# In the head, GpSimd takes the low part of the first half of each weight piece

## The reference, cut to what matters

```python
mod = silu(c) @ mod_w + mod_b                 # shift, scale and gate, 2048 each
h = rms_norm(x, gain) * (1 + scale) + shift
u, v = split(gelu(h @ w_in), 2)               # w_in: 2048 x 8192
v = rms_norm(v, v_gain)                       # then mixed over tokens by w_s, masked to be causal
```

## Time and profile before

| | us |
|---|---|
| median of 3 runs | 2571.34 (2571.24 to 2572.14) |
| the profiled execution, its own time | 2566.57 |
| its span, first to last instruction | 2564.8 |
| TensorE (PE) busy | 2492.9, 97% |
| VectorE (DVE) busy | 2131.3, 83% |
| ScalarE (ACT) busy | 1241.6, 48% |
| GpSimd (POOL) busy | 339.2, 13% |

### The profile page before, as it was taken

The page is one execution under the profiler, slowest core; times in us unless marked ns, Lnnn a source line. Parts: engine busy times, 40 slices in busy tenths (PEclk is TensorE's granted clock), DMA queues, the critical chain, the costliest instruction groups (busy, mean ns, idle before and its releaser), DMA issues.

```text
span 2564.8 us, 38496 instructions
## 1 busy us (share of the span) xinstructions
PE 2492.9 (97%) x14006; PEld 2151.4 (84%) x14006; DVE 2131.3 (83%) x2587; ACT 1241.6 (48%) x1644; POOL 339.2 (13%) x190
## 2 busy tenths in 40 slices
PE   6999999998999999999999999899999999999999
PEld 4877888887888888888887888688788888888887
DVE  7899898999999889988998788679999756765666
ACT  3437343544554355534544344573555445543553
POOL 0000110231120011101130000363122001200110
PEclk8999999999999999999999999999999999999999
DMA  9999688886878877787777879208677655555554
GB/s 369 364 359 345 252 338 328 321 325 257 310 283 305 331 293 290 290 339 291 274 268 279 313 277 351 99 18 327 239 287 292 223 189 190 187 189 188 181 180 148
DMA packets 94023, 685.49 MB, mean 267 GB/s; under 512 B 10433, under 2 KB 10433, under 8 KB 11201
## 3 DMA queue, kind: packets, MB, share of 16 engines
q1 hardware_dynamic: 93170, 677.08, 70.4%
q10 hardware_dynamic: 720, 6.57, 0.6%
HBM read 681.51 MB, written 2.10 MB: 267 GB/s over the span
## 4 chain that ended last, share of the span: by engine, by line
PE 75%; DVE 8%; DMA 3%; issue 2%; ACT 2%; POOL 1%; DVEq 0%; SPq 0%; ACTq 0%
PE banks L1504 48%; PE banks L1508 24%; DMA raw<-in_stream 3%; DVE w_lo L1109 2%; POOL attn_area L700 1%; DVE raw L1125 1%; ACT w_hi L935 1%; DVE scratch L865 1%; DVE attn_area L663 0%; PE banks L1492 0%; DVE x_res L1227 0%; PE banks L796 0%; DVE temp L1251 0%; DVE zpad L1246 0%; PE banks L1523 0%
## 5 line engine op out<-in xcount | busy, mean ns | idle before, releaser
L935 ACT ACTIVATE w_hi<-raw 128x1024 fp32r<-128x1024 f32 x833 | 866.9, 1056 | 990.8 <-PE banks L1508 569.3
L1109 DVE TENSOR_TENSOR w_lo<-raw,w_hi 128x1024 fp32r<-128x1024 f32 x833 | 1079.7, 1318 | 315.8 <-ACT w_hi L935 313.1
L1504 PE MATMUL banks<-h_op,w_hi 128*128 128x512 f32 x3808 | 1197.1, 396 | 5.7 <-DVE w_lo L1109 5.0
L1508 PEld LDWEIGHTS banks<-h_op,w_lo 128*128 128x128 f32 x3808 | 715.4, 188 | 169.1
L1508 PE MATMUL banks<-h_op,w_lo 128*128 128x256 f32 x3808 | 748.2, 278 | 0.0
L1504 PE MATMUL banks<-act_op,w_hi 128*128 128x512 f32 x2176 | 683.9, 396 | 0.8 <-DVE act_op L1269 0.5
L1504 PEld LDWEIGHTS banks<-h_op,w_hi 128*128 128x128 f32 x3808 | 579.7, 189 | 7.4 <-issue 4.6
L1125 DVE CUSTOM_DVE_ANT_0 raw<-raw,c_all 128x2048 f32<-128x2048 f32 x224 | 544.5, 2447 | 15.4 <-ACT c_all L909 9.6
L1508 PEld LDWEIGHTS banks<-act_op,w_lo 128*128 128x128 f32 x2176 | 408.8, 188 | 96.6
L1508 PE MATMUL banks<-act_op,w_lo 128*128 128x256 f32 x2176 | 427.5, 278 | 0.0
L1504 PEld LDWEIGHTS banks<-act_op,w_hi 128*128 128x128 f32 x2176 | 331.2, 189 | 1.7 <-DVE w_lo L1109 0.9
(11 more groups left out here) (159 smaller groups left out, 1312.3 us busy)
## 6 DMA issues: line engine op xcount, KB each, us to landing
raw<-in_stream SPq DMA_DIRECT2D x641, 1024.0 KB, 5.7
mix_area<-in_cmp_w ACTq DMA_DIRECT2D x2, 2048.0 KB, 11.7
x_res<-in_x SPq DMA_DIRECT2D x1, 2048.0 KB, 11.4
out_x<-x_res SPq DMA_DIRECT2D x4, 512.0 KB, 4.5
mix_area<-in_w_s ACTq DMA_DIRECT2D x1, 1024.0 KB, 10.2
mix_area<-in_b_s ACTq DMA_DIRECT2D x1, 1024.0 KB, 14.8
small<-in_small SPq DMA_DIRECT2D x1, 682.0 KB, 16.3
attn_area<-in_pos ACTq DMA_DIRECT2D x1, 273.0 KB, 5.3
```

The lines of the kernel that those rows point to most:

```text
L935: act.activation(w_hi[:, out, 0:n], raw[:, slot, half:half + n], ACT.Copy).then_inc(hi_ready, 1)
L1109: dve.tensor_tensor(w_lo[:, out, 0:n], raw[:, slot, half:half + n], w_hi[:, out, 0:n].bitcast(F32), ALU.subtract).then_inc(stream, 2 if ch ...
L1504: pe.matmul(banks[:, g + j, :], hi[:, k, P * j:P * (j + 1)], operand[:, kt, :], start=(kt == 0), stop=False, skip_group_check=True)
L1508: last = pe.matmul(banks[:, g + j, 0:T], lo[:, k, P * j:P * (j + 1)], operand[:, kt, 0:T], start=False, stop=(kt == last_kt), skip_group_c ...
```

## The change

In the head, `split_lo` on VectorE skips the first half of each weight piece (u even), and for the second half adds 2 to `stream`, so that a whole piece counts at once. GpSimd makes the low part of the first half, after `hi_ready`, and counts on a new semaphore `head_low`. TensorE waits for `head_low` ahead of a first half and for `stream` ahead of a second. The load of a piece waits for `stream` and, if the slot held a weight piece of the head, for `head_low` as well; for that the loads that follow pieces of the head are taken out of the loop and written out, with fixed addresses. The mask of `w_s` goes from ahead of GpSimd's steps to its first step of `sgu_u0`, behind the low parts.

```diff
@@ sync
+            head_pieces = BY_NAME["sgu_u0"][0].n["G"]
+            by_pool = [0] * head_pieces
+            for ch in BY_NAME["head"]:
+                for off, piece_kind in enumerate(ch.kinds_of):
+                    if piece_kind == "w":
+                        by_pool[ch.n["G"] + off] = 4 * ch.hs + ch.kinds_of[:off].count("w") + 1
             full = n_pieces // RAW_SLOTS
-            with sp.Fori(1, full) as i:
+            in_head = head_pieces // RAW_SLOTS + 1
+            for g in range(RAW_SLOTS, in_head * RAW_SLOTS):
+                sp.wait_ge(stream, 2 * (g - RAW_SLOTS + 1))
+                if by_pool[g - RAW_SLOTS]:
+                    sp.wait_ge(head_low, by_pool[g - RAW_SLOTS])
+                sp.dma_start(raw[:, g % RAW_SLOTS, :], io["stream"][g * P:(g + 1) * P, :]) \
+                    .then_inc(raw_loaded[g % RAW_SLOTS], 16)
+            with sp.Fori(in_head, full) as i:
@@ vector, split_lo
+                in_head = PHASE_OF[id(cur.first)] == "head"
+                if in_head and u % 2 == 0:
+                    return
...
-                                  ALU.subtract).then_inc(stream, 2 if chunk.kind == "gate" else 1)
+                                  ALU.subtract).then_inc(stream, 2 if in_head or chunk.kind == "gate" else 1)
@@ gpsimd
-            pool.wait_ge(mix_loaded, 32)
-            pool.affine_select(out=w_sT, in_=w_sT, compare_op=ALU.is_ge, fill=0.0, base=0,
-                               pattern=[[0, SGU_G], [1, P]], channel_multiplier=-1).then_inc(masked, 1)
-
             def step(name, cur, prev, first):
+
+                if name == "head":
+                    for u in range(0, 8, 2):
+                        off = cur.first.piece_of[[i for i, t in enumerate(cur.first.tokens) if t == "s"][u]]
+                        slot, out = (cur.first.n["G"] + off) % RAW_SLOTS, (cur.first.n["S"] + u) % SPLIT_SLOTS
+                        pool.wait_ge(hi_ready, cur.first.n["S"] + u + 1)
+                        pool.tensor_tensor(w_lo[:, out, :], raw[:, slot, 0:SUB], w_hi[:, out, :].bitcast(F32),
+                                           ALU.subtract).then_inc(head_low, 1)
+                if name == "sgu_u0" and first:
+                    pool.wait_ge(mix_loaded, 32)
+                    pool.affine_select(out=w_sT, in_=w_sT, compare_op=ALU.is_ge, fill=0.0, base=0,
+                                       pattern=[[0, SGU_G], [1, P]], channel_multiplier=-1).then_inc(masked, 1)
@@ tensor
-                    pe.wait_ge(stream, cur.val(lambda c: 2 * (c.n["G"] + off) + u % 2 + 1))
+                    if name == "head" and u % 2 == 0:
+                        pe.wait_ge(head_low, 4 * cur.first.hs + u // 2 + 1)
+                    else:
+                        pe.wait_ge(stream, cur.val(lambda c: 2 * (c.n["G"] + off) + u % 2 + 1))
```

More of the change, by code:

```diff
@@ L353, in build @@
         hi_ready = sem("hi_ready")
+        head_low = sem("head_low")
         stream = sem("stream")
```

## The result

The changed kernel takes 2580.65 us (2579.34 to 2581.22) against 2571.33 us for the one before, a ratio of 1.0041 (95% interval 1.0029 to 1.0053): slower, by about 10 us. The ratios here are taken over all runs of both kernels, so they are not exactly the quotient of the two medians. Run again beside later kernels the ratio was 1.0053 (1.0040 to 1.0066). The profiled execution took 2579.65 us, its span is 2577.9, 13.1 more than before.

What follows compares the result with a forecast made beforehand. TensorE bounds the kernel, so only the head counts: 190.4 us shared path + 10 late pieces - 189.7 = +10.7, or 2577.3 profiled; 4.8 carried over to the median gives 2582 us. Own range 2572 to 2593; 8 in 10, 2572 to 2601.

Steps and rivals of the forecast that it cites:

- The price of the GpSimd operation: Head: each added GpSimd low part takes 2.21 us of a path shared with VectorE, against 1.14 replaced; full lock 2.41.
- The shared path: Head: low parts on both engines, modulation pieces and operand makings sum to 190.4 us in 189.7, additions covered; chance 0.64.
- The late pieces: Head: of 13.6 us VectorE waits for late weight pieces, three quarters, 10 us, stay; ends 0 and 14.
- the three makings: Head: three makings of the operand, each 8.67 us in place of 4.49 between modulation pieces, add 12.5 us.
- VectorE's standstill: Head sign: VectorE's low parts and modulation pieces stretched by some 2 us per pair, means above 1.3 and 2.3.
- relief: Rival, head: lock rarely bites, standstill under 1.14 us per operation; 11.5 us faster, 2560 us; chance 0.06.
- The replay: Head's first pairs stepped through: modulation piece ends at 46.0 (before 42.6), next half 47.1; slots return 1 to 3 us later.
- The loads' and TensorE's waits: Head: loads waiting for both engines add nothing; TensorE's later first half counts only at the start, 1.1 us inside the sum.
- The mask: Mask of w_s moved behind the head's low parts stops VectorE as long there: net zero, between -1.4 and +2 us.
- One to one: The head's lengthening or shortening shifts the long TensorE stretch from 270 to 2560 us as a whole; it absorbs nothing.
- the transfers: Rival, head: transfers set the pace at a 357 GB/s ceiling; 0 to +4 us, taken as 2573; chance 0.14.
- let in late: Rival, head: GpSimd operations wait for VectorE's and take 6.56 us each; +33 us, 2604; chance 0.16.

Runs made afterwards that it cites:

- the three later series: Follow-up experiments, each run against the kernel before on the same chip; that kernel measured 2566.43, 2566.34 and 2567.54 us.
- where it was isolated: Kernel before plus one GpSimd subtraction per head pair on unrelated data, result unused, only the mask waiting for it: 2613.94 us, ratio 1.0187.
- the two split kernels: Changed kernel with GpSimd low parts only in the 10 head pairs with additions (2563.78 us, 0.9993 to kernel before), or only in the 22 others (2578.11, 1.0050).
- the kernel that was only late: VectorE makes all low parts; TensorE and loads wait for a GpSimd memset after the first one: 2571.70 us, ratio 1.0018 to the kernel before.

## Why the prediction was right

The forecast was +10.7 us, 2582; the timed medians give +9.3, the profiled spans +13.1, and the medians beside the later kernels +13.9. So the loss is some 9 to 14 us, and direction and size were right. That 2582 and 2580.65 lie so near is in part luck: the forecast was carried over to a median of the kernel before, 2571.34, that stood 4 to 5 us above its medians in the three later series (2566.34 to 2567.54). By its steps:

- *The price of the GpSimd operation*, 2.21 us: 2.20 where it was isolated, not the whole 2.41.
- *The shared path*, 32 x 5.56 + 12.5 = 190.4 us: pairs in a row took 5.52 (41.52 to 47.04). With additions they took 5.55, 5.56 and 5.55:

```profile
222.48 2.28 DVE L1142 CUSTOM_DVE_ANT_0 raw<-raw,c_all 128x2048 f32<-128x2048 f32 x1
224.69 1.28 DVE L1165 TENSOR_TENSOR scratch<-banks,scratch 128x512 f32<-128x512 f32 x2
225.89 2.21 DVE L1126 TENSOR_TENSOR w_lo<-raw,w_hi 128x1024 fp32r<-128x1024 f32 x1
228.03 2.28 DVE L1142 CUSTOM_DVE_ANT_0 raw<-raw,c_all 128x2048 f32<-128x2048 f32 x1
...
233.59 2.28 DVE L1142 CUSTOM_DVE_ANT_0 raw<-raw,c_all 128x2048 f32<-128x2048 f32 x1
...
239.14 4.09 DVE L1142 CUSTOM_DVE_ANT_0 raw<-raw,c_all 128x2048 f32<-128x2048 f32 x1
```

  These pairs are no longer with an addition than without: GpSimd covers it, as assumed. It does not do so in all ten: laid over each other, the timelines leave 3.6 us of additions, of 12.8 in the head, beside which GpSimd does not work. The prediction put this at nothing. Here the pairs were 5.7 to 6.3 us before, so this end of the head lost nothing, which the two split kernels confirm.
- *The late pieces*, 10 us of 13.6. From GpSimd's first low part (38.16) to 241.35, where the last modulation piece would have ended without the mask behind it (239.14 + 2.21), it is 203.2 us. Less 32 x 5.55 and 12.7 for the three makings (9.78 each from modulation piece to modulation piece, 5.55 without), 12.9 stay. The same overlay of the timelines tells what they are: for 8.2 us, outside the makings, neither engine works; 3.6 are the uncovered additions; 1.1 is not accounted for. The longest such wait, 170.98 to 173.04, stands behind an uncovered addition, VectorE's lines first:

```profile
169.69 1.28 DVE L1165 TENSOR_TENSOR scratch<-banks,scratch 128x512 f32<-128x512 f32 x2
174.01 2.46 DVE L1126 TENSOR_TENSOR w_lo<-raw,w_hi 128x1024 fp32r<-128x1024 f32 x1 [3.03 <-ACT w_hi L949]
...
173.04 2.35 POOL L1378 TENSOR_TENSOR w_lo<-raw,w_hi 128x1024 fp32r<-128x1024 f32 x1 [7.11 <-ACT w_hi L949]
```

  The 13.6 of the prediction were a little too many: three of the waits (0.34 each, behind the makings) are in the 12.5 for the makings as well, and two lie outside the stretch of 189.7 (0.34 at 38.09, 0.21 at 228.09), so 12.0 are left. Three quarters was a judgment; 8.2 of 12.0 is close to it. The term was 1.8 too large and the additions 3.6 too small, and the two partly cancel.
- *VectorE's standstill.* The prediction expected VectorE's operations stretched by some 2 us per pair. They were stretched by 1.1: 10.3 us on the modulation pieces (83.4 in place of 73.1) and 26.5 on the low parts (33 of them at 1.22 would be 40.3), less 1.8 for the mask, over 32 pairs. By the prediction's own words relief wins where the standstill is under 1.14, and there was none. The test was the wrong one: GpSimd's operation often runs while VectorE waits for `w_hi`, and then nothing stands still, but the path is taken all the same. VectorE's waits for `w_hi` went from 19.2 us to 35.6.
- *The replay* of the first pairs put the end of the first modulation piece at 46.0 and that of the next low part at 47.1; the trace has 45.97 (41.52 + 4.45) and 47.12 (45.90 + 1.22).
- *The loads' and TensorE's waits*, counted at nothing: in the changed kernel TensorE's split slots were no limit (ScalarE's 0.7 us). But the kernel that was only late lost some 5 us, so these waits are not free as such, as the prediction had it.
- *The mask*, net zero: it stopped the modulation piece of 239.14 for 1.8 us, where before it stopped a low part for 1.4; held back alone it made no difference that can be told.
- *One to one.* The delay of the head was passed on but for the 2.2 us that were made up behind it.
- *Rivals*: the transfers did not set the pace. Their share fell to 0.87, and 357 GB/s was no ceiling: with all low parts back on VectorE the same window moved 366.

```profile
38.00:230.00 192.00, 186.52 (x802) 152.58 (x803) 175.64 (x189) 97.73 (x140) 2.01 (x1) 0.97 0.95 366
```

  GpSimd was let in late in some pairs (at most 4.08 us, mean 2.92), never for 6.56. There was no relief except beside the additions.

## What to carry to other kernels

Moving work from VectorE to GpSimd takes it off VectorE's list, but not off the time that the two share: if VectorE's operations read two operands from SBUF and GpSimd's read SBUF too, the price is nearly GpSimd's whole time (2.20 us here), and this was twice VectorE's (1.14). Do not judge by VectorE's stretched operations alone: count the time in which either engine works. Before such a move, look in the trace for a GpSimd operation that already overlaps VectorE, and compare VectorE's duration there with its usual one. GpSimd work is cheap where VectorE reads from PSUM, or where GpSimd only writes; a piece no longer than VectorE's PSUM work can hide whole, if its data come in time.

## What the runs showed of the hardware

A GpSimd memset of 128x2304 f32 (2.03 us) beside VectorE's two-input operations held none of them, while a subtraction of 128x1024 of about the same length held them 2.20 us in each of the pairs shown. The mask, with one input, holds them too. VectorE's modulation piece of 47.04, which had begun half a microsecond before GpSimd's operation of 47.53, was finished first and not stretched.

Which engine goes first where both wait is not the same everywhere. At 41.6 us GpSimd's second low part, ready since the first was done, went ahead of VectorE's modulation piece. In the kernel before, the product recorded from 668.89 took 6.56 us while a low part and a modulation piece passed that VectorE began after it:

```profile
668.63 2.35 DVE L1109 TENSOR_TENSOR w_lo<-raw,w_hi 128x1024 fp32r<-128x1024 f32 x2
670.91 2.28 DVE L1125 CUSTOM_DVE_ANT_0 raw<-raw,c_all 128x2048 f32<-128x2048 f32 x1
...
673.12 4.55 DVE L1109 TENSOR_TENSOR w_lo<-raw,w_hi 128x1024 fp32r<-128x1024 f32 x2
```

What decides between the two is not shown by any run here.
